# Router logits taken ahead of the norm, stage tiles laid out as views of one room, and three expert panels loaded to other places

## The chip, the cores and the metric

One Trainium2 chip, one of its cores. The metric is the device time of one execution in microseconds (us). TensorE is called PE here, VectorE DVE, ScalarE ACT and SyncE SP; SP issues every DMA of this kernel, all on one queue.

## The reference, cut to what matters

The program is one transformer block with a mixture of experts, followed by two further layers. The change lies in the first block, with 256 tokens of width 1024:

```
x  = x + g1 * (m @ w_out)                  # m: the three branches, gated and merged
h2 = rms_norm(x, norm2_g) * (1 + sc2) + sh2
aff = softmax(h2 @ w_router)               # 256 tokens x 16 experts
top_w, top_i = top_k(aff.T, 32)            # every expert takes 32 tokens
xg = h2[top_i]
y  = (silu(xg @ w_gate) * (xg @ w_up)) @ w_down      # per expert
x  = x + g2 * scatter_add(y * top_w)
```

The two further layers (w_ada, w_ff1, ...) are untouched. All data is float32.

## The kernel before, in words

Everything is kept transposed: `xT` holds 8 tiles of 128 features by 256 tokens. Each engine has its own instruction list, written out in order, and waits on semaphores. A stage ends with a barrier of all engines.

**project_out** (lines 982 to 1145) merges the branches and applies `w_out`. PE makes 4 branch panels (L1071); DVE gates and adds them into `merged` (L1131 to L1137) and counts `bank_free`, which reaches 4 when the last gate is used. Then PE makes 8 chunks of the projection (L1770, 16 matrix instructions each), and DVE adds each into `xT` (L1777, count `x_updated`). PE's chunk q may start when chunk q-2 has been added. Between these additions DVE works on eight **side panels** (L1110 to L1117) of 1 MB each, which belong to the modulation of the next layer: the panel of number 4+q stands in DVE's list behind the addition of chunk q. SP loads them into three buffers (L1020), so panel 6 is issued when panel 3 is used up. After the last chunk come the norm's sum (L1651, L1653), the root on ACT (L1625), the reciprocal and scaling on DVE (L1668, L1674), the shift on ACT (L1659) and the router's logits on PE (L1086).

**moe** (line 1173 on) has 16 experts of 12 panels, each panel 2 MB of weights, 192 in all: 8 up panels (L1282) and 4 down panels (L1307) each. The first two panels lie in lead slots (`x_sel`'s room and `second_panel`), and 8 ring slots take the others in turn, so 10 panels fit before one has been used. `second_panel` is loaded once more. After that the panel of number r can be loaded when panel r-8 has been used. The opening is a chain: PE turns h (L1339), DVE and ACT make the softmax, DVE finds each expert's tokens (L1498 to L1512), PE gathers the tokens of four experts (L1355), and then the first up panel may start. The other experts' tokens are gathered between the up panels of the first expert (L1368); between its down panels PE makes 8 turns of the combine weights (L1332), each copied out by DVE (L1530) before the next.

## Time and profile before

| | |
|---|---|
| device time, median of 3 runs | 2592.0 us (2591.82 to 2593.31) |
| device time of the profiled execution | 2592.07 us |
| its span, first to last instruction | 2590.3 us |
| mean granted PE clock | 0.933 of 2.4 GHz |
| busy: PE, DVE, ACT | 2199.1, 1045.4, 470.3 us |
| DMA | 721.52 MB, mean 279 GB/s |
| issue of the router's load, SP L1024 | 256.51 us |
| span of the output projection's 8 chunks | from 281.94 us to 315.33 us |

Busy times of different engines overlap and say nothing of the end by themselves; which wait ends last in a stage is read from the timeline and the waits.

### The profile page before, as it was taken

The numbers are of one execution on the slowest core, as the hardware profiler recorded it, in microseconds if no ns is written. First come the engines' busy times: TensorE is split into PE (matmuls) and PEld (weight loads), VectorE is DVE, ScalarE is ACT, GpSimd is POOL, SyncE is SP. The second block draws the span as 40 slices with busy tenths as digits, with TensorE's granted clock in tenths as the row PEclk, the third lists the DMA queues.
The fourth block names the chain that finished last, engine by engine and source line by source line (L and its number), as shares of the span: only waits on it lengthen the run. The fifth ranks groups of instructions, "written<-read, shape, count | busy, mean of one in ns | idle before, by whom it ended". The sixth has DMA issues, their size and how long they took to land. (4 is left out here: it accounts for less than half of the span.)

```text
span 2590.3 us, 29682 instructions
## 1 busy us (share of the span) xinstructions
PE 2199.1 (85%) x11896; PEld 1519.2 (59%) x11896; DVE 1045.4 (40%) x1840; ACT 470.3 (18%) x1049; POOL 6.1 (0%) x11
## 2 busy tenths in 40 slices
PE   8999887566655565665899999999999999999998
PEld 5786742111111111111588886888888888778887
DVE  5753631000000100000587457576338754756531
ACT  3204110000000000000222045322112203442220
POOL 0000000000000000000000000000000000000000
PEclk9999988878888888778899999999999999999999
DMA  9653789999999999999977531076447663106430
GB/s 391 232 215 134 303 351 418 428 427 428 429 427 427 429 428 427 428 428 427 420 282 314 223 117 71 2 320 266 178 163 302 277 261 125 69 22 244 163 130 17
DMA packets 75202, 721.52 MB, mean 279 GB/s; under 512 B 8657, under 2 KB 11729, under 8 KB 13521
## 3 DMA queue, kind: packets, MB, share of 16 engines
q1 hardware_dynamic: 75088, 719.95, 67.8%
q8 instruction: 78, 1.28, 0.2%
q14 instruction: 36, 0.29, 0.0%
HBM read 718.87 MB, written 1.05 MB: 278 GB/s over the span
## 5 line engine op out<-in xcount | busy, mean ns | idle before, releaser
L1282 PE MATMUL bank<-pool,moe_x_cur 128*32 128x512 f32 x1776 | 266.3, 737 | 146.8 <-DMA pool<-in_w_expert 146.8
L1770 PE MATMUL bank<-trunk_proj,pool 128*128 128x256 f32 x1408 | 309.1, 379 | 0.0
L1770 PEld LDWEIGHTS bank<-trunk_proj,pool 128*128 128x128 f32 x1408 | 265.5, 190 | 37.5 <-issue 2.5
L1282 PEld LDWEIGHTS bank<-pool,moe_x_cur 128*32 128x32 f32 x1776 | 54.4, 122 | 344.6 <-DMA pool<-in_w_expert 238.8
L1307 PE MATMUL bank<-pool,moe_hidT 128*32 128x512 f32 x864 | 143.8, 802 | 72.7 <-DMA pool<-in_w_expert 65.2
L1468 DVE TENSOR_TENSOR moe_hid<-bank,moe_silu 128x512 f32<-128x512 f32 x16 | 11.1, 691 | 449.9 <-ACT moe_silu L1424 449.9
L1848 PE MATMUL bank<-pool 128*128 128x256 f32 x640 | 152.1, 381 | 0.0
L1848 PE MATMUL bank<-spare,trunk_mix 128*128 128x256 f32 x640 | 146.7, 382 | 3.6 <-ACT first_layer_sq L1907 3.6
L2156 PE MATMUL bank<-pool 128*128 128x256 f32 x672 | 148.3, 380 | 0.0
L1848 PE MATMUL bank<-pool,trunk_mix 128*128 128x256 f32 x640 | 145.7, 381 | 0.0
L2156 PEld LDWEIGHTS bank<-pool 128*128 128x128 f32 x672 | 127.2, 190 | 21.2 <-issue 4.2
L1848 PEld LDWEIGHTS bank<-spare,trunk_mix 128*128 128x128 f32 x640 | 122.6, 192 | 20.9 <-issue 4.0
L1848 PEld LDWEIGHTS bank<-pool,trunk_mix 128*128 128x128 f32 x640 | 122.5, 191 | 17.0
L1307 PEld LDWEIGHTS bank<-pool,moe_hidT 128*32 128x32 f32 x864 | 28.0, 131 | 172.8 <-DMA pool<-in_w_expert 105.6
L787 PE MATMUL bank<-pool 128*128 128x256 f32 x576 | 126.8, 379 | 1.0 <-PEq L2926 1.0
L1848 PEld LDWEIGHTS bank<-pool 128*128 128x128 f32 x640 | 117.6, 190 | 17.2 <-issue 3.3
L787 PEld LDWEIGHTS bank<-pool 128*128 128x128 f32 x576 | 109.2, 190 | 19.1 <-issue 4.7
L1472 DVE COPY moe_y<-bank 128x512 f32<-128x512 f32 x16 | 11.1, 691 | 264.4 <-PE bank L1307 247.8
L1424 ACT ACTIVATE moe_silu<-bank 128x512 f32<-128x512 f32 x16 | 9.6, 597 | 567.3 <-PE bank L1282 567.3
L1321 PE MATMUL bank<-moe_place,moe_y 128*128 (+1 forms) x256 | 70.1, 422 | 43.7 <-DVE xT L1481 26.3
L1777 DVE SCALAR_TENSOR_TENSOR xT<-bank,gain,xT 128x256 f32<-128x256 f32 x32 | 15.5, 484 | 214.8 <-PE bank L1770 214.8
L1321 PEld LDWEIGHTS bank<-moe_place,moe_y 128*128 128x128 f32 x256 | 50.4, 207 | 76.4 <-DVE xT L1481 33.2
(647 smaller groups left out, 2876.2 us busy)
## 6 DMA issues: line engine op xcount, KB each, us to landing
pool<-in_w_expert SPq DMA_DIRECT2D x165, 2048.0 KB, 35.7
pool<-in_w_ff SPq DMA_DIRECT2D x132, 1024.0 KB, 6.9
pool<-in_w_ada SPq DMA_DIRECT2D x66, 1024.0 KB, 8.9
moe_more<-in_w_expert SPq DMA_DIRECT2D x23, 2048.0 KB, 37.0
pool<-in_w_in SPq DMA_DIRECT2D x40, 1024.0 KB, 5.1
pool<-in_w_mod SPq DMA_DIRECT2D x24, 1024.0 KB, 7.8
pool<-in_w_out SPq DMA_DIRECT2D x10, 1024.0 KB, 10.4
pool<-in_small SPq DMA_DIRECT2D x2, 2560.0 KB, 9.4
```

The source lines that it names most:

```text
L787: mm = pe.matmul(ps[p % 3][:, j * T:(j + 1) * T], w[:, j * KD + k], h[:, k], start=k == 0, stop=k == KD - 1)
L1282: mm = pe.matmul(ps[b][quarter[g], :], x_cur[:, u], w[:, b, g], start=u == 0, stop=u == up_panels - 1)
L1307: mm = pe.matmul(ps[2 + b][quarter[g], :], hidT[:, s, g], w[:, g, b], start=s == 0, stop=s == down_panels - 1)
L1321: mm = pe.matmul(ps[at][:, (j % 2) * T:(j % 2 + 1) * T], y[:, k * P:(k + 1) * P], place_of[:, e], start=True, stop=True)
L1424: sc.activation(silu, ps[0], ACT.Silu).then_inc(silu_done, 1)
L1468: ve.tensor_tensor(hid, ps[1], silu, MUL).then_inc(hid_done, 1)
L1472: ve.tensor_copy(y[:, 512:D], ps[3]).then_inc(y_high, 1)
L1770: mm = pe.matmul(self.ps[3 + q % 2][:, 0:T], w, x[:, k], start=k == 0, stop=k == nk - 1)
L1777: ve.scalar_tensor_tensor(self.xT[:, q], self.ps[3 + q % 2][:, 0:T], gain[:, q:q + 1], self.xT[:, q], MUL, ADD).then_inc(self.x_updated, 1)
L1848: mm = pe.matmul(bank, left[:, k], right[:, k], start=start and k == 0, stop=k == 3, skip_group_check=True)
L2156: mm = pe.matmul(ps[n % 3][:, j * T:(j + 1) * T], slot[:, j * KD + k], hT[:, k], start=k == 0, stop=k == KD - 1)
```

## The change

1. **project_out.** The router works on `x * gain`, which DVE writes as each chunk is added (`dve_lead`); the logits of features 0 to 3 stand in PE's list behind chunk 4, the others behind chunk 7. The token's 1/rms and the shift's part of the logits are applied later, to 16 numbers a token. The sum of squares goes to a column per token (8 small matrix instructions of one column). The router's load is issued first. ACT takes one square root early, and loads the table for Exp at the end.
2. **Room.** The tiles of front, project_in, project_out and moe are views of one tile, `room`. This frees the places of `x_sel` and `more` when the gates are merged, and two panels (0 and 9) are loaded there inside project_out, at `bank_free` 4, ahead of side panels 6 and 7 in SP's list.
3. **moe.** An eleventh panel (number 10) goes into h's buffer when h has been turned. The reload of `second_panel` becomes number 11. The tokens and h are scaled and shifted where they are copied out. The combine weights are no longer spread fourfold by ACT: PE's turns of them become 16 matrix products with 32-column weights, in place of 4 transposes. Two copies of the affinities are left out (DVE reads PSUM).

```diff
@@ project_out, SP
+                sp.dma_start(router, I["small1"][:, SM1["router"][0]:SM1["router"][1]]).then_inc(router_here, 16)
                 for n in range(len(side)):
                     side_panel(n)
-                sp.dma_start(router, I["small1"][:, SM1["router"][0]:SM1["router"][1]]).then_inc(router_here, 16)
...
                     if u == 3:
+                        sp.wait_ge(d.bank_free, panels)
+                        for slot, n, here in early_panels:
+                            sp.dma_start(slot, I["w_expert"][0, n]).then_inc(here, 16)
                         for n in range(len(side) + panels - 1, 8):
                             side_panel(n)
@@ project_out, PE
+                def logits(k):
+                    pe.wait_ge(d.led, k + 1)
+                    for t in range(NT):
+                        pe.matmul(ps[t][:, 0:E], h[:, k, t * P:(t + 1) * P], router[:, k * E:(k + 1) * E],
+                                  start=k == 0, stop=k == KD - 1)
...
+                    if q == 4:
+                        for k in range(4):
+                            logits(k)
+                for k in range(4, KD - 1):
+                    logits(k)
+
+                pe.wait_ge(d.folded, 6)
+                pe.wait_ge(d.squared, KD)
+                for t in range(NT):
+                    col = slice(t * P, (t + 1) * P)
+                    pe.matmul(ps[6][:, t:t + 1], d.rstd[:, col], c["ones"][:, 0:1], start=True, stop=False)
+                    mm = pe.matmul(ps[6][:, t:t + 1], d.sq[:, 3, col], c["ones"][:, 0:1], start=False, stop=True)
+                mm.then_inc(d.summed, 1)
+                logits(KD - 1)
@@ project_out, ACT and DVE
-                d.act_norm(sc, 0, mod[:, 24:32, 0], 1)
+                sc.wait_ge(d.summed, 1)
+                sc.activation(root, ps[6][:, 0:NT], ACT.Sqrt, bias=c["eps"][:, 0:1], scale=1.0 / D).then_inc(d.rooted, 1)
+                sc.activation(folded_shift[:, 0:NT], c["eps"][:, 0:NT], ACT.Exp)
-                    d.dve_add(ve, q, 0, mod[:, 16:24, 0], d, 0)
+                    d.dve_add(ve, q, 0, mod[:, 16:24, 0], d, 0, gain[:, 2])
-                d.dve_norm(ve, 0, gain[:, 2])
@@ moe
-                sp.dma_start(lead_slots[0], src[0, 0]).then_inc(lead_here[0], 16)
-                for u in range(6, slots):
-                    sp.dma_start(slot[u], src[0, u + leads]).then_inc(slot_loaded[u], 16)
+                sp.dma_start(slot[6], src[0, 6 + leads]).then_inc(slot_loaded[6], 16)
+                sp.wait_ge(h_turned, 4)
+                sp.dma_start(h_room, src[0, in_h]).then_inc(h_room_here, 16)
                 sp.wait_ge(panel_done, 2)
                 sp.dma_start(second_panel, src[0, again]).then_inc(second_here, 16)
                 for r in range(again + 1, 2 * n):
-                    sp.wait_ge(panel_done, r - slots if r <= again + slots else r - slots + 1)
+                    sp.wait_ge(panel_done, r - slots - 1 if r <= again + slots else r - slots + 1)
...
-                        mm = pe.transpose(ps[7][:, j * P:(j + 1) * P],
-                                          w_tok[:, j % 2, 2 * g + j // 2].rearrange("p a b -> p (a b)"), c["ident"])
+                        for rows in quarter:
+                            mm = pe.matmul(ps[7][rows, j * P:(j + 1) * P], w_tok[:, j % 2, 2 * g + j // 2], c["ident"],
+                                           start=True, stop=True)
...
-                ve.tensor_copy(affT, ps[1][0:E, 0:T])
-                link(ve.tensor_copy(left, ps[1][0:E, 0:T]))
```

The helper that `gain[:, 2]` switches on, unchanged in the file:

```
    def dve_add(self, ve, q, n, gain, norm, m, lead_gain=None):
        if q >= 2 and lead_gain is not None:
            norm.dve_fold(ve, m, q - 1)
        self.dve_update(ve, q, n, gain)
        if lead_gain is not None:
            ve.wait_ge(self.x_updated, n + q + 1)
            norm.dve_lead(ve, q, lead_gain)
```

On SP, in project_out from the first expert panel to the end of the stage, before and after (`room` is where the side panels' tiles, and now two expert panels, lie; `in_w_ada` is the side panels' source, `in_w_expert` the experts'):

```order
L1039 DMA pool<-in_w_expert 128x4096
L1020 DMA mixer_proj<-in_w_ada 128x2048
L1020 DMA mixer_spec<-in_w_ada 128x2048
L1020 DMA pool<-in_w_ada 128x8x256
L1039 DMA pool<-in_w_expert 128x4096 x2
L1020 DMA mixer_proj<-in_w_ada 128x2048
L1020 DMA mixer_spec<-in_w_ada 128x2048
L1039 DMA pool<-in_w_expert 128x4096 x3
```

```order
L1046 DMA pool<-in_w_expert 128x4096
L1024 DMA first_room<-in_w_ada 128x2048 x2
L1024 DMA pool<-in_w_ada 128x8x256
L1046 DMA pool<-in_w_expert 128x4096 x2
L1040 DMA first_room<-in_w_expert 128x4096 x2
L1024 DMA first_room<-in_w_ada 128x2048 x2
L1046 DMA pool<-in_w_expert 128x4096 x3
```

Two loads of 2 MB (L1040) now stand between the panels issued at 282.30 us and side panels 6 and 7.

On PE, from the projection's chunk 3 to the end of the stage before, and to the sum of squares now (L1770 and L1811 are the same chunks, 8 products each; L1086 and L1072 the logits; L1651, L1653 and L1107, L1108 the sum of squares; L1096 the shift's part of the logits):

```order
L1770 MATMUL bank<-pool 128x256 x32
L1049 MATMUL bank<-mixer_kv,ones 32x256 x4
L1770 MATMUL bank<-pool 128x256 x8
L1651 MATMUL bank<-pool,ones 128x256
L1653 MATMUL bank<-pool,ones 128x256
L1059 MATMUL bank<-ident,project_out_rows 128x128 x2
L1086 MATMUL bank<-first_router,pool 128x16 x16
```

```order
L1811 MATMUL bank<-pool 128x256 x8
L1096 MATMUL bank<-pool,ones 128x16
L1811 MATMUL bank<-pool 128x256 x8
L1072 MATMUL bank<-first_router,pool 128x16 x8
L1811 MATMUL bank<-pool 128x256 x16
L1056 MATMUL bank<-first_room,ones 32x256 x4
L1811 MATMUL bank<-pool 128x256 x8
L1066 MATMUL bank<-ident,project_out_rows 128x128 x2
L1072 MATMUL bank<-first_router,pool 128x16 x6
L1107 MATMUL bank<-ones,pool 128x1
L1108 MATMUL bank<-ones,pool 128x1
```

Half of the 16 products of the logits moved between chunk 4 and chunk 5. Six stand behind chunk 7; then the pair L1107, L1108 comes for each of two tiles of tokens, and the last two products follow.

On PE, in the first expert's down panels, before and now (L1307 and L1346 are the panels, L1332 and L1372 the turns of the combine weights, two turns each row):

```order
L1307 MATMUL bank<-pool,moe_hidT 32x512 x8
L1332 MATMUL bank<-ident,pool 128x128 x8
L1307 MATMUL bank<-moe_more,moe_hidT 32x512 x8
L1332 MATMUL bank<-ident,pool 128x128 x8
L1307 MATMUL bank<-spare,moe_hidT 32x512 x8
```

```order
L1346 MATMUL bank<-pool,first_room 32x512 x8
L1372 MATMUL bank<-ident,first_room 32x128 x32
L1346 MATMUL bank<-first_room 32x512 x8
L1372 MATMUL bank<-ident,first_room 32x128 x32
L1346 MATMUL bank<-pool,first_room 32x512 x8
```

Each pair of turns went from 8 instructions to 32; the third panel is now the one in h's buffer.

## Rows read from the trace of the kernel before

**Rows 1.** The page, GB/s of DMA in 40 equal slices of the span
```profile
GB/s 391 232 215 134 303 351 418 428 427 428 429 427 427 429 428 427 428 428 427 420 282 314 223 117 71 2 320 266 178 163 302 277 261 125 69 22 244 163 130 17
```

**Rows 2.** Windows: stretch, its us, busy us by engine, PEclk, DMA share, GB/s
```profile
400.00:405.00 5.00, 5.00 (x49) 1.59 (x52) 1.66 (x4) 0.00 (x0) 0.00 (x0) 1.00 0.83 288
405.00:1245.00 840.00, 514.05 (x3099) 139.53 (x3092) 66.56 (x142) 32.01 (x60) 0.00 (x0) 0.82 1.01 428
345.00:350.00 5.00, 4.63 (x36) 1.90 (x38) 1.66 (x3) 3.02 (x3) 0.00 (x0) 1.00 0.02 7
```

**Rows 3.** Longest of PE's waits inside the expert stage, 405 to 1245 us
```profile
PE bank L1282 <- DMA pool<-in_w_expert: 146.8, 67, 3.0
```

**Rows 4.** Timeline of SP's issues around the output projection
```profile
282.30 1.13 SPq L1039 DMA_DIRECT2D pool<-in_w_expert  x2
288.60 0.33 SPq L1020 DMA_DIRECT2D mixer_proj<-in_w_ada  x1
...
298.62 17.55 SPq L1039 DMA_DIRECT2D pool<-in_w_expert  x3
```

**Rows 5.** DMA issues of 288.4 to 291.2 us: KB each, us to landing
```profile
mixer_proj<-in_w_ada SPq DMA_DIRECT2D x1, 1024.0 KB, 12.3
```

**Rows 6.** DMA issue of 283.0 us alone, then that of 298.6 us
```profile
pool<-in_w_expert SPq DMA_DIRECT2D x1, 2048.0 KB, 15.4
...
pool<-in_w_expert SPq DMA_DIRECT2D x1, 2048.0 KB, 9.6
```

**Rows 7.** Timeline of DVE, 300 to 304 us
```profile
300.89 1.28 DVE L1114 SCALAR_TENSOR_TENSOR mixer_kv<-mixer_proj,cond,mixer_kv 128x1024 f32<-128x1024 f32 x1 [5.11 <-DMA mixer_proj<-in_w_ada]
...
303.41 0.48 DVE L1777 SCALAR_TENSOR_TENSOR xT<-bank,first_mod,xT 128x256 f32<-128x256 f32 x1
```

**Rows 8.** Timeline of PE from chunk 0 of the projection to the expert stage
```profile
286.12 4.58 PE L1770 MATMUL bank<-pool 128*128 128x256 f32 x20 [1.42 <-DVE pool L1137]
...
303.94 7.17 PE L1770 MATMUL bank<-pool 128*128 128x256 f32 x32 [1.89 <-DVE xT L1777]
...
311.61 3.72 PE L1770 MATMUL bank<-pool 128*128 128x256 f32 x16
...
321.09 6.98 PE L1086 MATMUL bank<-first_router,pool 128*128 128x16 f32 x32 [3.49 <-ACT pool L1659]
328.36 3.29 PE L1339 MATMUL bank<-ident,pool 128*128 128x128 f32 x16 [0.30 <-PEq L1007]
```

**Rows 9.** Timeline of ACT, 328 us
```profile
328.32 1.28 ACT L1437 ACT_TABLE_LOAD   x1 [4.40 <-PEq L1007]
```

**Rows 10.** Windows of PE's lower clock, columns as in Rows 2
```profile
320.90:331.20 10.30, 9.81 (x46) 9.77 (x47) 3.40 (x13) 5.89 (x17) 0.00 (x0) 0.50 0.76 285
...
339.40:344.80 5.40, 5.35 (x25) 5.38 (x26) 2.04 (x4) 0.28 (x1) 0.00 (x0) 0.50 0.98 422
```

**Rows 11.** Timeline of DVE in the routing
```profile
330.54 0.37 DVE L1495 TENSOR_SCALAR moe_aff<-moe_e,moe_tot 128x16 f32<-128x16 f32 x2
331.91 0.41 DVE L1498 COPY moe_y<-bank 16x256 f32<-16x256 f32 x1 [1.00 <-PE bank L1344]
...
332.69 0.42 DVE L1501 MAX8 moe_best<-moe_y 16x8 f32<-16x256 f32 x1
...
338.81 1.43 DVE L1512 TENSOR_TENSOR moe_place<-moe_placeT,moe_numbers 128x128 f32<-128x128 f32 x4
```

**Rows 12.** Timeline of PE, first panel of the first expert
```profile
346.18 1.92 PE L1282 MATMUL bank<-moe_x_sel,moe_x_cur 128*32 128x512 f32 x16 [0.37 <-ACT moe_x_cur L1445]
```

**Rows 13.** DMA issue of 315.7 us: KB, us to landing
```profile
pool<-in_w_expert SPq DMA_DIRECT2D x1, 2048.0 KB, 13.5
```

**Rows 14.** Timeline of PE in the first expert's down panels
```profile
380.57 0.66 PE L1332 MATMUL bank<-ident,pool 128*128 128x128 f32 x4 [0.78 <-DVE moe_place L1530]
```

**Rows 15.** PE and its weight loads with 32-column weights
```profile
290.63 0.64 PE L1049 MATMUL bank<-mixer_proj,ones 128*32 128x256 f32 x8
...
346.18 0.16 PEld L1282 LDWEIGHTS bank<-moe_x_sel,moe_x_cur 128*32 128x32 f32 x8 [0.56 <-ACT moe_x_cur L1445]
```

More of the change, by code:

```diff
@@ L992, in project_out @@
         merging, router_here, gain_squared = st.sem("merging"), st.sem("router_here"), st.sem("gain_squared")
+        shift_rows, shift_sum, shift_made = st.sem("shift_rows"), st.sem("shift_sum"), st.sem("shift_made")
+        d.lead, d.led_before = h, {0: 0}
+        by_shift = d.silu[:, 0, 0:KD * E].rearrange("p (k e) -> p k e", k=KD)
+        folded_shift, root = d.silu[:, 1, 0:E], d.root[:, 0:NT]
         panels, x_gain = 4, t["x_gain"]
@@ L1147, in _ @@
                         tile_add(0)
-                d.dve_norm(ve, 0, gain[:, 2])
                 tile_add(1)
+                ve.wait_ge(d.rooted, 1)
+                ve.reciprocal(route["rstd"], root)
 def head_rows_of(extra):
@@ L1173, in moe @@
 def moe(nc, c, ps, cst, hT, place_of, x_sel, slot, slot_loaded, src, xT, gate, pool, w_ff, ff_here, x_gain, second_panel,
-        second_here, ff_mod, ff_gain, final_g):
+        second_here, ff_mod, ff_gain, final_g, route, shift, lead_sem, take):
     up_panels, down_panels = KD, 4
@@ L1187, in moe @@
         e1 = st.sb("e1", [P, NT, E])
+        logits = st.sb("logits", [P, NT, E])
         top = st.sb("top", [P, NT])
@@ L1271, in panel @@
                         return second_panel
-                    if opening and r < again:
+                    if opening and r == in_h:
+                        pe.wait_ge(h_room_here, 16)
+                        return h_room
+                    if opening and r < in_h:
                         pe.wait_ge(slot_loaded[r - leads], 16)
                         return slot[r - leads]
-                    pe.wait_ge(slot_loaded[slot_of(r)], i * (32 * n // slots) + ((r - leads - 1) // slots + 1) * 16)
+                    pe.wait_ge(slot_loaded[slot_of(r)], i * (32 * n // slots) + ((r - leads - 2) // slots + 1) * 16)
                     return slot[slot_of(r)]
@@ L1420, in tokens, with middle @@
                     sc.activation(x_cur, xs[:, :, e], ACT.Copy).then_inc(x_ready, 1)
-                def middle(e, more):
+                def middle(e, more, opening=False):
                     sc.wait_ge(panel_done, e * n + up_panels)
@@ L1432, in middle @@
                     sc.wait_ge(panel_done, e * n + n)
+                    if opening:
+                        sc.wait_ge(w_turned, E // 2)
                     sc.activation(y[:, 0:512], ps[2], ACT.Copy).then_inc(y_low, 1)
                 for t in range(NT):
-                    sc.wait_ge(highest, NT)
-                    sc.activation(e1[:, t], ps[t][:, 0:E], ACT.Exp, bias=top[:, t:t + 1],
+                    sc.wait_ge(highest, 1)
+                    sc.activation(e1[:, t], logits[:, t], ACT.Exp, bias=top[:, t:t + 1],
                                   accum_out=tot[:, t:t + 1]).then_inc(exped, 1)
@@ L1489, in _ @@
                 for t in range(NT):
-                    ve.tensor_reduce(top[:, t:t + 1], ps[t][:, 0:E], AX.X, MAX, negate=True).then_inc(highest, 1)
+                    m = ve.scalar_tensor_tensor(logits[:, t], ps[t][:, 0:E], route["rstd"][:, t:t + 1], route["shift"], MUL, ADD)
+                link(m)
+                ve.tensor_reduce(top, logits, AX.X, MAX, negate=True).then_inc(highest, 1)
                 link(ve.memset(zero, 0.0))
@@ L2790, with __init__ @@
 class Spectrum:
-    def __init__(self, st, c, ps, cst, src, vec, spec):
+    def __init__(self, st, c, ps, cst, src, vec, spec, take):
         self.c, self.ps, self.cst, self.src, self.vec, self.spec = c, ps, cst, src, vec, spec
-        self.small = st.sb("small", [P, SM1["router"][0]])
-        self.feats = st.sb("feats", [P, T])
-        self.window = st.sb("window", [P, NT, T])
-        self.dft = st.sb("dft", [P, 4, 640])
-        self.masked = st.sb("masked", [P, P])
-        self.h1 = st.sb("h1", [HEAD, T])
-        self.ang = st.sb("ang", [HEAD, T])
-        self.tmp = st.sb("tmp", [HEAD, T])
-        self.filt = st.sb("filt", [P, NT, 2, 512])
-        self.size = st.sb("size", [P, NT, 2, 512])
-        self.norm = st.sb("norm", [P, 512])
+        self.small = take(SM1["router"][0])
+        self.feats = take(T)
+        self.window = take(NT, T)
+        self.dft = take(4, 640)
+        self.masked = take(P)
+        self.h1 = take(T, rows=HEAD)
+        self.ang = take(T, rows=HEAD)
+        self.tmp = take(T, rows=HEAD)
+        self.filt = take(NT, 2, 512)
+        self.size = take(NT, 2, 512)
+        self.norm = take(512)
         self.first_here, self.later_here, self.layer, self.angled, self.sined = (
@@ L2896, in dve_divide, with front @@
             ve.tensor_tensor(self.spec[:, f], self.ps[1 + f], self.norm, MUL)
-def front(nc, c, ps, ring, extra, I, cst, vec, cond, xT, ctxT, hT, mod, gain, spec, slots, loaded, consts, consts_here):
+def front(nc, c, ps, ring, extra, I, cst, vec, cond, xT, ctxT, hT, mod, gain, spec, slots, loaded, consts, consts_here, take):
     v = lambda k: vec[:, V1[k][0]:V1[k][1]]
```

117 lines of the change are left out of this document (64 added, 53 removed).

## The prediction

> **What bounds the kernel now.** I read the page first: from slice 7 to slice 20, near half the span, DMA moves 418 to 429 GB/s [rows 1]. So I cut the expert stage into windows: from 405 to 1245 us the DMA share is 1.01 at 428 GB/s, while PE is busy for 514 of 840 us [rows 2], and the longest of PE's waits there is for expert panels, 146.8 us in 67 waits [rows 3]. A panel of 2,097,152 bytes costs 2.097 / 0.428 = 4.9 us of that stream. The 192 panels pass through a fixed number of places, so time is lost or won only where the stream pauses or starts. It starts in the stage's opening, when 10 panels are loaded and the first has not been used: between 345 and 350 us it moves 7 GB/s [rows 2]. There is a second weak spot, 400 to 405 us with 288 GB/s. The load of panel 20 may be issued only when panel 12 has been used, the first of the second expert, and so behind the whole first expert on PE. Every microsecond by which PE comes later to panel 12 moves the rest of the stream, and the end, by one microsecond. I therefore followed PE and what it waits for from the output projection to there.
>
> **The two early panels.** SP issued two expert panels at 282.30 and 283.0 us, side panel 6 at 288.60 [rows 4]. The second of the two landed 15.4 us after its issue, at 298.4 [rows 6], side panel 6 12.3 us after its own, at 300.9 [rows 5], the panel issued at 298.62 9.6 us later, at 308.2 [rows 6]. All land in the order of issue, and back to back. DVE stood 5.11 us for side panel 6 and began with it at 300.89 [rows 7]. Behind it in DVE's list is the addition of chunk 3, which ended at 303.89, and PE's chunk 5 waits for that: it began at 303.94 [rows 8]. Now two panels of 4.9 us are issued at `bank_free` 4, just ahead of 286.12, where PE's wait on DVE's last gate ends [rows 8]; side panel 6 still waits for panel 3's use, to 288.6. So it stands behind 9.8 us more of DMA and lands at 310.7.
> From there: side panel 6 on DVE 2.6 us (300.89 to the addition's 303.41 is 2.52) to 313.3; `dve_add` now folds a square first and writes `dve_lead` afterwards. The trace ahead of the change has no lead here; I price fold and lead as the addition beside them, 0.48 each at most [rows 7], pipelined to some 0.4. The addition ends at 314.2, lead 3 at 314.6. Logits 0 to 2 fit into PE's wait; those of feature 3 do not, 4 instructions of 6.98 / 32 = 0.22 us [rows 8], 0.9 us. Chunk 5 begins at about 315.5, **11.5 us later**. In that gap PE would have little to do. After its thin stretch ahead of 320.9 the granted clock was 0.50 (1.2 GHz), for 10.3 us; in the gather it came back 5.4 us after 339.4 [rows 10]. I take 5.4 us at half speed, which costs 2.7 us (bounds: 0 without a fall, 5.2 with 10.3 us of it). Chunks 5 to 7 took from 303.94 to 315.33 [rows 8]; so chunk 7 ends at 315.5 + 11.4 + 2.7 = 329.5, 14.2 later.
>
> **The norm's tail.** From 315.33 to the first instruction of moe at 328.36 were 13.0 us: sum, root, reciprocal, scaling, shift, 32 instructions of logits [rows 8]. What remains: one turn of 0.35, 12 instructions of logits, 8 of the column sums, a root of 128x2, then on ACT the table load of 1.28, which stood in moe at 328.32 [rows 9], and an Exp of 0.3. The 0.22 us of a product with 128-column weights was at clock 0.50 [rows 8, 10]; behind three busy chunks I take 0.11. So 0.35 + 12 x 0.11 + 8 x 0.11 + 0.2 + 0.3 + 1.28 + 0.3, and 0.2 for the barrier, is 4.8 us (at the lower clock 7.0). The saving is 8.2 us. moe starts at 334.3, **6.0 later**.
>
> **The opening of moe.** The affinities were ready at 330.91 and PE's 16 transposes of h, 3.29 us at the lower clock, held them up until 331.6; then two copies ran from 331.91 to the first MAX8 at 332.69 [rows 8, 11]. The copies go: 0.8 us. The table load is gone ahead of the Exp; with the transposes at full clock (1.8 us) the affinities go through 1.0 us sooner, at the lower clock not at all. I take 1.8 together. Against it: `numbers` was used at 338.81 [rows 11], and its load now queues behind the panels issued at chunk 7's end. The second of that pair landed 13.5 us after its issue [rows 13]: 329.8 + 13.5 = 343.3, where DVE wants it at 334.3 + 10.5 - 1.8 = 343.0. I take 0.5 us (bounds 0 and 1.5). The first up panel, 346.18 before [rows 12], comes 6.0 - 1.8 + 0.5 = **4.7 later**, at 350.9. Additions and scalings that replace copies (`x_cur`, `x_sel`, h's copy) have the shapes of the copies; I give them nothing, for DVE is busy there for 1.66 of 5 us [rows 2], and ACT's four copies of h end long before the gather. ACT's spread lay beside PE's up panels; its absence brings nothing.
>
> **The turns of the combine weights.** A turn of 4 transposes took 0.66 us, and the next waits 0.78 for DVE's copy [rows 14]; all 8 stand in PE's chain to panel 12. Now 32 instructions with 32-column weights. The nearest rows: 16 such instructions of 512 columns take 1.92 us [rows 12], 8 of 256 columns 0.64 [rows 15]. Four run together, so these are 4 rounds and 2 rounds; a line through both gives 0.21 us plus 0.83 ns a column, so 8 rounds of 128 columns take 1.07. That is 0.41 more each, **3.3 us** for eight. The bounds: nothing (as now) and 32 x 0.08 = 2.6 us each, if an instruction costs what it does in the 256-column row whatever its length, 15 us more in all.
> A rule speaks for something like the upper bound. The Trainium skill (TensorE: Matmul & The Clock Gate, Part 3: Packing small matmuls) says that weight loads overlap running matmuls only when the row group differs; these quarters differ in columns only. By it 32 loads of 0.106 us would stand in line and a turn would be an estimated 3.4 us. The trace does not agree: 8 loads of this kind lie within 0.16 us [rows 15].
>
> **The eleventh panel.** It would take 4.9 us off the stream if the stream ran on. But panels 11 to 19 now fill the 9 places that come free early, and panel 20 still waits for panel 12. From panel 2's use to the end of 19 are 9 panels instead of 10, so the pause ahead of 20 grows by the 4.9 us that were won. I count nothing. The later issue of the feed-forward panels at the stage's end (the turn of the slots shifts by one) I count at nothing too: they queue behind the last expert panels, which PE itself still waits for.
>
> **The sum.** 11.5 + 2.7 - 8.2 - 1.8 + 0.5 + 3.3 = 8.0 us later at panel 12, and so at the end. The profiled execution took 2592.07 around a span of 2590.3; the median is 2592.0. Forecast: **2600 us**.
>
> **Rivals.**
> (a) The side panels are not held up. If the DMA engines let the 1 MB loads past, chunk 5 starts at about 305.0 (fold, lead, logits of feature 3), chunk 7 ends at 316.4, moe starts at 321.2, the first up panel at 337.8, 8.4 earlier, and with 3.3 for the turns the end is 5.1 earlier: 2587. For it speaks only that 16 engines each work on their own share, of which these landings show the last alone; against it, that each load of these 25 us landed in the order of issue [rows 4 to 6]. It decides from this point: if side panel 6 comes less than about 5 us later, the change does not lose. By the Trainium skill (DMA: Bandwidth & Descriptors, Queues, rings and completion order) an engine takes up descriptors in ring order; by that rule, the trace agrees. Chance 0.07.
> (b) The stream and not PE decides at panel 20. Then the eleventh panel counts: 4.7 - 4.9, no change, 2592. Against it: panel 2 is used some 5 us after 350.9, panel 19 lands 9 x 4.9 us and a start of 2 or 3 later, at some 403 us; the load of 20 was issued in the weak spot from 400 to 405 us [rows 2], and PE now gets there 8 us later. Chance 0.08.
> (c) PE's clock stays up through the wait, or comes back before the gather: the 2.7 falls away, and the gather of 6.4 us at the lower clock halves. 2594 to 2597. Chance 0.18.
> (d) A turn costs an instruction's 0.08 or the rule's load 32 times: 2600 + 12 to + 19, 2612 to 2619. Chance 0.06.
> The forecast's own course has 0.61.
>
> **Range.** The forecast's own bounds: clock -2.7 and +2.5, tail +2.2, numbers -0.5 and +1.0, not all at once: 2595 to 2606. With (c), and the lower side for (b), 2592 to 2606 holds 8 in 10. A measurement of this kernel tells about 0.2%, 5.2 us. Faster by that needs (a) at its full size: 0.06. Within it lie (b), most of (c) and the low edge of the forecast: 0.24. Slower: 0.70.
>
> **What would show it.** Of the kernel after: DVE waits some 15 us for side panel 6 and starts it near 310.7; PE's chunk 5 begins near 315, at clock 0.50; from chunk 7's end to moe 5 us; the first up panel near 351; a turn of 32 instructions near 1.1 us; DMA nearly still for 6 to 7 us ahead of panel 20, and 428 GB/s from there. Wrong would be: side panel 6 at its old time, a DMA without that pause, or turns of over 1.5 us.

## The result, and the profile after

| | before | after |
|---|---|---|
| median of 16 runs each | 2592.53 us (2587.83 to 2594.64) | 2598.29 us (2597.17 to 2601.74) |
| span of the profiled execution | 2590.3 us | 2596.5 us |

The ratio is 1.0027, with a 95% interval from 1.002 to 1.0033: the change makes the kernel slower by 5.8 us. Measured again (e11 below), the same two kernels gave 1.003 (1.0018 to 1.0042). The forecast was 2600.0 us.

The page of the kernel after, GB/s of DMA in 40 slices. The plateau of 427 to 428 stands where it stood, with the same height; the slices ahead of it changed (351 and 418 were slices 6 and 7 in [rows 1], now 341 and 369), and so did those behind its end:

```profile
GB/s 391 232 213 136 320 341 369 427 427 428 428 428 428 428 428 428 428 428 427 420 302 291 250 114 73 2 307 266 190 162 292 278 262 130 65 26 243 163 130 17
```

SP's issues, timeline (start, length, queue, line). The pair of L1040 stands ahead of the two side panels of L1024, which are issued at the time of [rows 4]:

```profile
282.42 1.13 SPq L1046 DMA_DIRECT2D pool<-in_w_expert  x2
286.21 0.81 SPq L1040 DMA_DIRECT2D first_room<-in_w_expert  x2
288.73 3.10 SPq L1024 DMA_DIRECT2D first_room<-in_w_ada  x2
298.75 31.84 SPq L1046 DMA_DIRECT2D pool<-in_w_expert  x3
```

DMA issues of 288.5 to 289 us: KB each, us to landing. It was 12.3 in [rows 5]:

```profile
first_room<-in_w_ada SPq DMA_DIRECT2D x1, 1024.0 KB, 22.3
```

DVE's timeline. The number in brackets is the wait ahead of the instruction; it was 5.11 in [rows 7]. Behind the side panel come the addition of chunk 3 (L1818) and the scaled copy for the router (L1727):

```profile
311.10 1.28 DVE L1143 SCALAR_TENSOR_TENSOR first_room<-first_room,cond 128x1024 f32<-128x1024 f32 x1 [15.15 <-DMA first_room<-in_w_ada]
...
313.96 0.48 DVE L1818 SCALAR_TENSOR_TENSOR xT<-bank,first_mod,xT 128x256 f32<-128x256 f32 x1
314.48 0.35 DVE L1727 TENSOR_SCALAR pool<-xT,first_gain 128x256 f32<-128x256 f32 x1
```

PE's timeline over the same stretch, to the first up panel:

```profile
302.23 1.41 PE L1072 MATMUL bank<-first_router,pool 128*128 128x16 f32 x12
314.88 1.04 PE L1072 MATMUL bank<-first_router,pool 128*128 128x16 f32 x4 [11.24 <-DVE pool L1727]
315.76 9.78 PE L1811 MATMUL bank<-pool 128*128 128x256 f32 x32
...
326.03 3.72 PE L1811 MATMUL bank<-pool 128*128 128x256 f32 x16
...
329.81 1.41 PE L1072 MATMUL bank<-first_router,pool 128*128 128x16 f32 x12
...
334.21 3.17 PE L1379 MATMUL bank<-ident,pool 128*128 128x128 f32 x16 [1.65 <-PEq L1011]
...
344.61 5.61 PE L1395 MATMUL bank<-first_room 128*128 128x128 f32 x32 [0.91 <-DVE first_room L1548]
350.60 1.92 PE L1321 MATMUL bank<-first_room,moe_x_cur 128*32 128x512 f32 x16 [0.38 <-DVE moe_x_cur L1558]
```

PE stands 11.24 us for the copy, starts chunk 5 at 315.76 (before: 303.94), and chunks 5 and 6 take 9.78 us where they took 7.17 [rows 8]. Chunk 7 ends at 329.75, moe starts 4.46 us later. The first window below shows why the two chunks are slow (columns: us; busy us of PE, PEld, DVE, ACT, POOL; granted clock; DMA share; GB/s): the clock is at its lower level, 0.50 or 1.2 GHz, for 13.7 us, from 3.8 us into PE's wait on. The second window shows the pause ahead of panel 20, the third the stream behind it:

```profile
307.40:321.10 13.70, 6.22 (x17) 5.14 (x18) 7.71 (x12) 2.49 (x5) 0.00 (x0) 0.50 0.65 272
...
404.00:410.00 6.00, 4.86 (x36) 2.37 (x40) 2.74 (x7) 0.00 (x0) 0.00 (x0) 1.00 0.00 0
409.00:1250.00 841.00, 522.23 (x3116) 140.35 (x3108) 66.61 (x142) 32.02 (x60) 0.00 (x0) 0.81 1.01 427
```

ACT's timeline at the end of the output projection: root, table load and Exp end at 333.9, and the barrier lets moe start at 334.21. DVE's timeline in moe follows, where `numbers` is first used at L1548, with no wait ahead of it:

```profile
332.14 0.26 ACT L1129 ACTIVATE pool<-bank,eps 128x2 f32<-128x2 f32 x1 [1.41 <-PE bank L1108]
332.42 1.28 ACT L1130 ACT_TABLE_LOAD   x1
333.71 0.20 ACT L1130 ACTIVATE pool<-eps 128x2 f32<-128x2 f32 x1
```

```profile
337.84 0.42 DVE L1537 MAX8 moe_best<-bank 16x8 f32<-16x256 f32 x1 [1.63 <-PE bank L1384]
...
343.96 1.43 DVE L1548 TENSOR_TENSOR first_room<-moe_placeT,moe_numbers 128x128 f32<-128x128 f32 x4
```

PE's timeline in the first expert's down panels (L1346) with the turns (L1372), and the first half of the tokens' return (L1360):

```profile
383.73 1.08 PE L1372 MATMUL bank<-ident,first_room 128*32 128x128 f32 x32 [0.81 <-DVE first_room L1571]
384.63 1.90 PE L1346 MATMUL bank<-first_room 128*32 128x512 f32 x16
386.35 1.06 PE L1372 MATMUL bank<-ident,first_room 128*32 128x128 f32 x32
...
389.12 1.90 PE L1346 MATMUL bank<-pool,first_room 128*32 128x512 f32 x16
...
399.88 3.51 PE L1360 MATMUL bank<-first_room 128*128 128x256 f32 x8 [1.61 <-DVE first_room L1506]
```

The same stretch in the kernel before (L1307 are the down panels, L1321 the tokens' return):

```profile
375.68 3.52 PE L1307 MATMUL bank<-pool,moe_hidT 128*32 128x512 f32 x16 [0.69 <-ACT moe_hidT L1431]
...
381.16 1.92 PE L1307 MATMUL bank<-moe_more,moe_hidT 128*32 128x512 f32 x16
...
385.04 1.92 PE L1307 MATMUL bank<-spare,moe_hidT 128*32 128x512 f32 x16
...
394.45 1.97 PE L1321 MATMUL bank<-moe_place,moe_y 128*128 128x256 f32 x8 [1.58 <-DVE moe_y L1472]
```

A turn takes 1.08 us (0.66 in [rows 14]), but two panels follow each other 4.49 us apart instead of 3.88, so a turn costs the chain 0.3 us. Panel 20 was issued at 409.05 and landed 8.9 us later, at 417.9; before it was issued at 402.07 and landed at 410.0. Panel 19 had landed at 404.0, and at 404.4 before: the stream hardly paused before (5.5 us between the two landings, 4.9 is back to back) and clearly does now (13.9 us).

Two executions of one kernel do not agree in every stage. A second profile of the kernel after (e11 below) begins with the same instructions at the same times, but its clock is at the lower level from 36.6 to 43.4 us, and from 40 us on it runs 3.0 to 3.2 us later:

```profile
36.60:43.40 6.80, 6.10 (x23) 2.70 (x24) 3.28 (x12) 2.67 (x7) 0.00 (x0) 0.50 1.01 416
```

The first profile has 1.00 there. Of the 13 profiles, those of e4, e8 and e11 have this stretch (6.8 us) and those of e1 and e7 half of it (3.4 us, 1.3 us later from there on). It lies in the first stage, far ahead of project_out and moe. Where experiments are compared, times are therefore also given from **the gate**, the start of PE's row behind its wait for DVE's last gate (286.12 in [rows 8], at the end of chunk 0; 286.24 in the kernel after, 289.40 in e11).

### The profile page after: what moved, and what is told of

It reads as the page before. It is cut to its first block and busy times, and to the rows that moved or that the text cites. A ratio compares the mean times of both kernels' runs of the same rounds, so it can differ in the third digit from the quotient of the medians.

```text
span 2596.5 us, 30125 instructions
## 1 busy us (share of the span) xinstructions
PE 2204.2 (85%) x12126; PEld 1521.0 (59%) x12126; DVE 1045.7 (40%) x1843; ACT 464.6 (18%) x1039; POOL 6.1 (0%) x11
## 5 line engine op out<-in xcount | busy, mean ns | idle before, releaser
L1321 PE MATMUL bank<-pool,moe_x_cur 128*32 128x512 f32 x1776 | 265.7, 735 | 138.7 <-DMA pool<-in_w_expert 138.7
L1811 PE MATMUL bank<-trunk_proj,pool 128*128 128x256 f32 x1408 | 309.1, 379 | 0.0
L1811 PEld LDWEIGHTS bank<-trunk_proj,pool 128*128 128x128 f32 x1408 | 265.5, 190 | 37.5 <-issue 2.5
L1321 PEld LDWEIGHTS bank<-pool,moe_x_cur 128*32 128x32 f32 x1776 | 54.2, 122 | 333.8 <-DMA pool<-in_w_expert 227.8
L1346 PE MATMUL bank<-pool,first_room 128*32 128x512 f32 x864 | 146.2, 815 | 71.5 <-DMA pool<-in_w_expert 63.4
L1502 DVE TENSOR_TENSOR first_room<-bank,first_room 128x512 f32<-128x512 f32 x16 | 11.1, 691 | 448.0 <-ACT first_room L1464 448.0
L2197 PEld LDWEIGHTS bank<-pool 128*128 128x128 f32 x672 | 127.2, 190 | 21.2 <-issue 4.2
L1346 PEld LDWEIGHTS bank<-pool,first_room 128*32 128x32 f32 x864 | 28.1, 132 | 173.1 <-DMA pool<-in_w_expert 108.2
L1506 DVE COPY first_room<-bank 128x512 f32<-128x512 f32 x16 | 11.1, 691 | 266.1 <-PE bank L1346 249.5
L1464 ACT ACTIVATE first_room<-bank 128x512 f32<-128x512 f32 x16 | 9.6, 597 | 565.1 <-PE bank L1321 565.1
L1360 PE MATMUL bank<-first_room 128*128 (+1 forms) x256 | 71.8, 430 | 43.7 <-DVE xT L1515 26.3
L1818 DVE SCALAR_TENSOR_TENSOR xT<-bank,gain,xT 128x256 f32<-128x256 f32 x32 | 15.5, 484 | 214.7 <-PE bank L1811 214.7
L1360 PEld LDWEIGHTS bank<-first_room 128*128 128x128 f32 x256 | 51.5, 211 | 77.8 <-DVE xT L1515 33.4
```

What stands on the lines that cost most here:

```text
L1321: mm = pe.matmul(ps[b][quarter[g], :], x_cur[:, u], w[:, b, g], start=u == 0, stop=u == up_panels - 1)
L1346: mm = pe.matmul(ps[2 + b][quarter[g], :], hidT[:, s, g], w[:, g, b], start=s == 0, stop=s == down_panels - 1)
L1360: mm = pe.matmul(ps[at][:, (j % 2) * T:(j % 2 + 1) * T], y[:, k * P:(k + 1) * P], place_of[:, e], start=True, stop=True)
L1464: sc.activation(silu, ps[0], ACT.Silu).then_inc(silu_done, 1)
L1502: ve.tensor_tensor(hid, ps[1], silu, MUL).then_inc(hid_done, 1)
L1506: ve.tensor_copy(y[:, 512:D], ps[3]).then_inc(y_high, 1)
```

## The experiments

Eleven kernels ran, the last of them the kernel after again. The median of the kernel before beside them was 2590.9 us for the first eight and 2592.0 us for the last three. Read from one profile each, in us from the gate:

| | first up panel | issue of panel 20 | landing of panel 22 | last instruction |
|---|---|---|---|---|
| before | 60.1 | 116.0 | 133.6 | 2304.2 |
| after | 64.4 | 122.8 | 141.5 | 2310.3 |
| e11, after again | 63.8 | 120.7 | 139.4 | 2310.2 |
| e1 | 54.0 | 112.6 | 131.2 | 2302.0 |
| e2 | 59.2 | 117.5 | 136.0 | 2304.8 |
| e3 | 64.2 | 122.8 | 141.3 | 2312.1 |
| e4 | 63.8 | 118.1 | 136.7 | 2306.5 |
| e5 | 54.7 | 95.2 | 122.8 | 2294.4 |
| e6 | 64.4 | 104.8 | 132.5 | 2304.1 |
| e7 | 54.1 | 100.8 | 127.2 | 2298.4 |
| e8 | 53.1 | 93.6 | 124.6 | 2296.2 |
| e9 | 67.2 | 125.7 | 144.4 | 2314.9 |
| e10 | 52.7 | 94.8 | 120.9 | 2292.9 |

**The place of the early panels.** In e1_behind both stand behind side panels 6 and 7, in e2_half one ahead and one behind. The edit of e1:

```diff
                     if u == 3:
-                        sp.wait_ge(d.bank_free, panels)
-                        for slot, n, here in early_panels:
-                            sp.dma_start(slot, I["w_expert"][0, n]).then_inc(here, 16)
                         for n in range(len(side) + panels - 1, 8):
                             side_panel(n)
+                        sp.wait_ge(d.bank_free, panels)
+                        for slot, n, here in early_panels:
+                            sp.dma_start(slot, I["w_expert"][0, n]).then_inc(here, 16)
```

> The changed kernel with one edit: SP issues the two early expert panels behind side panels 6 and 7 instead of ahead of them. Theory A (the early panels hold up side panel 6, and PE's arrival at panel 12 sets the end): DVE starts side panel 6 near 301 us instead of 311, the projection's chunk 5 starts near 305, the first up panel near 338, the load of panel 20 is issued near 396 us instead of 409, and the time falls by about 13 us, to 2585 to 2587, 5 to 7 us below the kernel before. Theory B (the expert stream itself decides, and the early panels' place matters little): within 2 us of the changed kernel's 2598.

> The changed kernel with one of the two early panels ahead of side panels 6 and 7 and the other behind them: half the dose. Theory A: side panel 6 lands 4.9 us earlier than in the changed kernel, near 306 us, chunk 5 starts near 310.5, and the time is about 5 us less plus what the clock gives back (0 to 3 us): 2590.5 to 2593.5. Theory B: 2597 to 2599. If the loss were a matter of the two panels' contention and not of their place in line, the time would stay near 2598 too.

Measured: e1 2588.44 us (2585.37 to 2591.36), ratio 0.999 (0.9981 to 0.9999); e2 2595.09 us (2592.08 to 2595.47), ratio 1.0014 (1.0005 to 1.0023). DVE's wait in e1, then PE's first work of chunk 5 and the gather:

```profile
302.48 1.28 DVE L1143 SCALAR_TENSOR_TENSOR first_room<-first_room,cond 128x1024 f32<-128x1024 f32 x1 [5.22 <-DMA first_room<-in_w_ada]
```

```profile
306.98 8.57 PE L1811 MATMUL bank<-pool 128*128 128x256 f32 x32
...
334.49 6.71 PE L1395 MATMUL bank<-first_room 128*128 128x128 f32 x32 [0.90 <-DVE first_room L1548]
341.58 1.92 PE L1321 MATMUL bank<-first_room,moe_x_cur 128*32 128x512 f32 x16 [0.38 <-DVE moe_x_cur L1558]
```

The same wait in e2:

```profile
306.19 1.28 DVE L1144 SCALAR_TENSOR_TENSOR first_room<-first_room,cond 128x1024 f32<-128x1024 f32 x1 [10.19 <-DMA first_room<-in_w_ada]
```

DVE waits 5.22, 10.19 and 15.15 us with no, one and two panels ahead: 5.0 us each, the time of 2 MB. From the gate the issue of panel 20 comes after 112.6, 117.5 and 122.8 us, 4.9 and 5.3 apart. So the order in SP's list is the cause of the loss: with it put right, the rest of the change is worth some 2.5 us by both medians and ratio, with an interval from 0.3 to 4.9. e1 gave back 10 us where 13 were expected, and missed its range of 2585 to 2587 by 1.4 us. Most of the rest is the clock: chunks 5 and 6 of e1 still took 8.57 us, 1.4 more than before, and its gather 6.71, 1.1 more than the 5.61 of the kernel after. e2 missed its range by 1.6 us: by the ratios it is 3.4 us below the kernel after and not 5, though its profile shows the 5 us at panel 20.

**The eleventh panel and the turns.** e3_no_eleventh reloads `second_panel` for panel 10, as before. e4_no_eleventh_old_turns also has the 4 transposes a turn and ACT's spread.

```diff
@@ e3
-        in_h = leads + slots
-        again = in_h + 1
+        again = leads + slots
...
-                sp.wait_ge(h_turned, 4)
-                sp.dma_start(h_room, src[0, in_h]).then_inc(h_room_here, 16)
...
@@ e4, further
...
-                        for rows in quarter:
-                            mm = pe.matmul(ps[7][rows, j * P:(j + 1) * P], w_tok[:, j % 2, 2 * g + j // 2], c["ident"],
-                                           start=True, stop=True)
+                        mm = pe.transpose(ps[7][:, j * P:(j + 1) * P],
+                                          w_tok[:, j % 2, 2 * g + j // 2].rearrange("p a b -> p (a b)"), c["ident"])
...
```

> The changed kernel without the eleventh panel: nothing is loaded into h's buffer, panel 10 goes to second_panel again as in the kernel before, the rest of the change stays. Theory A (the load of panel 20 waits for PE at panel 12, so an eleventh place only lengthens the pause ahead of 20): no change, 2597 to 2599.5, with the stream's pause ahead of panel 20 shorter by about 4.9 us. Theory B (each place ahead takes a panel of 4.9 us off the stream): 2603.

> As e3_no_eleventh, and the combine weights are spread fourfold by ACT and turned by 4 transposes as in the kernel before. Theory A with the turns' price of 0.42 us each: PE is 3.4 us sooner at panel 12; panel 19 lands near 409 us, so the stream allows 3 to 4 us: 2594 to 2595.5, 3 to 4 us below e3_no_eleventh. If the turns are hidden (the rival): equal to e3_no_eleventh within 1 us.

Measured: e3 2600.18 us (2599.53 to 2601.6), ratio 1.0037 (1.0023 to 1.0051); e4 2596.7 us (2592.85 to 2598.29), ratio 1.0019 (1.001 to 1.0028). The window of e3 ahead of panel 20, columns as above, against 0 GB/s in the kernel after:

```profile
404.00:410.00 6.00, 4.89 (x36) 2.37 (x40) 2.71 (x7) 0.00 (x0) 0.00 (x0) 1.00 0.49 202
```

In e3 panel 19 lands at 409.1 instead of 404.0, but panel 20 is issued at 409.0 and lands at 417.7 instead of 417.9: the eleventh place only lengthens the pause. The median of e3 lies 0.7 us above its range of 2597 to 2599.5 and 2 us above the kernel after; the landings do not show this, and the intervals of the two ratios overlap. In e4 a turn's row is 0.66 us again, and the four down panels with their turns take 15.6 us (382.48 to 398.07) instead of the 18.1 of the kernel after (380.12 to 398.27). The new turns cost 2.5 us in all. The medians of e3 and e4 are 3.5 us apart, and panel 20's issue 4.6 us from the gate, but the clock has a part in this: the first down panel of e3 took 3.51 us at the lower clock, that of e4 1.92.

```profile
389.65 0.66 PE L1366 MATMUL bank<-ident,pool 128*128 128x128 f32 x4 [0.79 <-DVE first_room L1570]
390.24 1.92 PE L1341 MATMUL bank<-spare,first_room 128*32 128x512 f32 x16
```

**Reusing the places.** If the pause ahead of panel 20 is where the extra places go lost, their reload should bring them back. In e5_behind_reuse (with e1's order) h's buffer takes panel 20 when panel 10 has been used, `second_panel` takes 21 when 11 has been used, and the ring goes on with 22. e6_reuse is this edit without e1's order.

```diff
...
+                sp.wait_ge(panel_done, in_h + 1)
+                sp.dma_start(h_room, src[ring // n, ring % n]).then_inc(h_room_here, 16)
+                sp.wait_ge(panel_done, again + 1)
+                sp.dma_start(second_panel, src[(ring + 1) // n, (ring + 1) % n]).then_inc(second_here, 16)
+                for r in range(ring + 2, 2 * n):
+                    sp.wait_ge(panel_done, r - slots - 1)
...
```

> e1_behind with one edit more: panels 20 and 21 go once more into h's buffer and second_panel (free when panels 10 and 11 are used), so the load of 20 no longer waits for PE at panel 12; the ring slots go on from panel 22. Theory A (in e1_behind the stream stands idle ahead of panel 20 because the place comes free only with panel 12): panel 21 lands near 405 us and 22 near 410, instead of 418.8 for panel 22 in e1_behind, the pause is gone, and the time falls by 8 to 9 us, to 2579 to 2581. Rival (the pause is harmless, or PE is the bound in the second expert): within 2 us of e1_behind's 2588.4.

> The changed kernel with that edit alone; the early panels stay ahead of the side panels. Theory A: panel 22 lands near 418.5 us instead of 427.7, and the time is 9 us below the changed kernel's, 2589 to 2590, no slower than the kernel before although PE is as late as ever. Rival: 2597 to 2599.

Measured: e5 2582.89 us (2580.12 to 2585.8), ratio 0.997 (0.9958 to 0.9982), the lowest time so far; e6 2592.08 us (2590.1 to 2595.81), ratio 1.0004 (0.9995 to 1.0013). Windows of e5: the stream runs through where e1 and the kernel after stood still.

```profile
390.00:396.00 6.00, 4.00 (x10) 2.75 (x11) 1.66 (x4) 0.00 (x0) 0.00 (x0) 0.72 1.02 434
396.00:402.00 6.00, 6.00 (x52) 2.55 (x54) 1.66 (x4) 0.00 (x0) 0.00 (x0) 1.00 1.04 429
```

In e1, whose gate lies 1.3 us later, 6 us out of the same stretch:

```profile
394.00:400.00 6.00, 4.25 (x31) 2.16 (x33) 3.32 (x8) 0.00 (x0) 0.00 (x0) 1.00 0.01 3
```

From the gate, panel 22 landed after 122.8 us in e5 and 131.2 in e1, after 132.5 in e6 and 141.5 in the kernel after: 8.4 and 8.9 us sooner, about as theory A had it. The end came 7.6 and 6.2 us sooner in the profiles, and in time the reload is worth 5 us from e1 to e5 and 6 us from the kernel after to e6, each by the ratios times 2592. That is less than the 8 to 9 us expected, and both runs lie some 2 us above their ranges. What was given back between panel 22 and the end was not traced. Without the reload the eleventh place showed nothing (e3).

**What each place is then worth.** e7_behind_reuse_no_eleventh is e5 without the eleventh panel. e8_no_early_reuse is e5 with the two early panels loaded when moe starts.

```diff
@@ e7, on e5: h's buffer takes no panel
-                sp.wait_ge(h_turned, 4)
-                sp.dma_start(h_room, src[0, in_h]).then_inc(h_room_here, 16)
...
@@ e8, on e5
...
-                        for slot, n, here in early_panels:
-                            sp.dma_start(slot, I["w_expert"][0, n]).then_inc(here, 16)
...
+                sp.dma_start(lead_slots[0], src[0, 0]).then_inc(lead_here[0], 16)
+                for u in range(6, slots):
+                    sp.dma_start(slot[u], src[0, u + leads]).then_inc(slot_loaded[u], 16)
```

> e5_behind_reuse without the eleventh panel: panel 10 goes to second_panel, which is loaded a third time with panel 19; nothing lies in h's buffer. Theory A: the stream has no pause in either, so here, unlike in e3_no_eleventh, the eleventh place counts as one panel of the stream: 4.9 us above e5_behind_reuse, 2584 to 2586. Rival (the eleventh place is worth nothing at all): equal to e5_behind_reuse within 1 us.

> As e5_behind_reuse, but panels 0 and 9 are not loaded early: they go to the same places at the start of the expert stage, as in the kernel before. Theory A: the stream still carries them between 327 and 352 us, where it otherwise stands nearly still, panel 11 lands near 357 us instead of 354.6, and the time is 2 to 3 us above e5_behind_reuse: the two early panels are worth far less than their 9.8 us. Rival: 9 to 10 us above e5_behind_reuse.

Measured: e7 2586.0 us (2580.7 to 2588.03), ratio 0.9974 (0.9965 to 0.9984); e8 2585.68 us (2582.33 to 2587.05), ratio 0.9978 (0.9969 to 0.9987). From the gate, panel 22 lands after 122.8 us in e5, 127.2 in e7 and 124.6 in e8. The eleventh panel is worth 4.4 us of landing and 4.0 us at the end of the profile, the early loads 1.7 and 1.8 us. In time they are 3.1 and 2.8 us by medians, 1.0 and 2.1 us by the ratios; the intervals of e5, e7 and e8 overlap, so the times do not show the size of either, and it rests on one profile of each.

**The clock and the wait.** e9_busy_wait puts 40 products on PE into its wait for side panel 6; e10_busy_opening puts 5 and 18 on e5's PE, in the barrier's wait and in the routing's. e11_after_again is the kernel after, unedited.

```diff
@@ e9
                     if q == 4:
-                        for k in range(4):
+                        for k in range(3):
                             logits(k)
+                        for _ in range(40):
+                            pe.matmul(ps[6][:, 0:T], c["ident"], merged[:, 0], start=True, stop=True)
+                        logits(3)
@@ e10, on e5, behind the last logits and behind the transposes of the affinities
+                for _ in range(5):
+                    pe.matmul(ps[5][:, 0:T], c["ident"], xT[:, 0], start=True, stop=True)
...
+                for _ in range(18):
+                    pe.matmul(ps[7][:, 0:T], c["ident"], xT[:, 0], start=True, stop=True)
```

> The changed kernel, with 40 extra products (128 rows by 256 columns, result not used) on PE inside its 11.2 us wait, ahead of the logits of feature 3. Theory (the thin stretch of PE sets the granted clock back, and the lower clock costs time in chunks 5 and 6 and later in the routing): the products run 302.9 to some 312, chunks 5 and 6 take 7.2 us instead of 9.8, the lower clock at 307.4 is gone, moe and the first up panel come 2.6 us earlier (348.0), the end some 2.6 us earlier: about 2595.5 where the changed kernel gives 2598. Rival (the granted clock falls by its own course, whatever PE does): chunks 5 and 6 still 9.8, time as before. Side panel 6 lands at 311.1 in both.

> The kernel with the early panels behind side panels 6 and 7 and the two reloads (2582.9), with extra products on PE whose result is not used: 5 behind the last logits of the output projection (in the barrier's wait) and 18 in PE's 5.5 us wait of the routing. Theory (the granted clock follows how busy PE is): the transposes of h take 1.8 instead of 2.8 us, the gather some 3 instead of 6.0, the first up panel comes 3 to 4 us earlier, at 337.5, and the end at about 2579.5. Rival (PE has to be busy for longer than these 6 us before the clock rises, or the extra products themselves run at the lower clock and then reach into the chain): 18 products at half speed take 8.3 us instead of the wait's 5.5, so the gather starts up to 2.8 us later: 2583 to 2586.

> The changed kernel itself, unedited, beside the other two on one chip: 2597 to 2599 by all theories; it is the base for the difference of the run with the busy wait.

Measured: e9 2603.02 us (2601.12 to 2604.03), ratio 1.0043 (1.0029 to 1.0057); e10 2582.34 us (2580.93 to 2583.98), ratio 0.9966 (0.9954 to 0.9978); e11 2599.6 us (2598.0 to 2601.42), ratio 1.003 (1.0018 to 1.0042). PE in e9:

```profile
303.57 17.51 PE L1101 MATMUL bank<-pool,ident 128*128 128x256 f32 x80
320.93 0.52 PE L1072 MATMUL bank<-first_router,pool 128*128 128x16 f32 x4
321.29 7.15 PE L1814 MATMUL bank<-pool 128*128 128x256 f32 x32
...
337.12 2.39 PE L1382 MATMUL bank<-ident,pool 128*128 128x128 f32 x16 [1.65 <-PEq L1011]
```

Here I sized the edit wrong. A product in float32 is two rows of the trace (x80 for 40), 0.44 us, so the products ran 17.5 us and not 9, and chunk 5 began 5.5 us later than in the kernel after. The run is useful all the same: chunks 5 and 6 take 7.15 us instead of 9.78, the lower clock of 307.4 us is gone, and all five profiles with PE's wait of 11 us and nothing in it (the kernel after, e3, e4, e6 and e11) have these chunks slow, 8.55 to 9.95 us. That speaks for the wait as what brings the lower clock; it is one profile of e9, and e10 below shows that the clock is not settled by PE's work alone. The sum 5.5 - 2.6 = 2.9 us is met: moe starts at 337.12 instead of 334.21 (from the gate 3.3 us later than in e11), and the median is 3.4 above e11. So a delay of PE ahead of the first expert shows at the end at about its size.

PE in e10, where the same error made the 18 products reach past DVE's result:

```profile
325.66 7.93 PE L1408 MATMUL bank<-xT,ident 128*128 128x256 f32 x36
333.52 0.29 PE L1411 MATMUL bank<-ident,first_room 16*128 16x16 f32 x2
334.72 3.81 PE L1418 MATMUL bank<-first_room 128*128 128x128 f32 x32 [0.90 <-DVE first_room L1571]
```

From moe's start the turn of the places came 1.4 us later than in e5 (10.1 us instead of 8.7), the gather took 3.81 instead of 5.97 us, and the first up panel came 0.8 us sooner. Against it, the 5 products in the barrier's wait took 3.58 us, most of it at the lower clock, and moe began 2.1 us later behind the last logits than in e5. In time the whole is nothing that the runs tell from e5, and neither the 2579.5 of the theory nor the rival's 2583 to 2586 was met. Whether fewer products would bring more was not tried.

The same two profiles show something else. Ahead of the 5 products at 319.5 us PE's instructions are the same in e5 and e10, and so is PE's wait of 1.3 us ahead of the logits of feature 3. Chunks 5 and 6 took 10.15 us in e5 and 7.15 in e10:

```profile
305.77 10.15 PE L1830 MATMUL bank<-pool 128*128 128x256 f32 x32
```

```profile
305.47 7.15 PE L1834 MATMUL bank<-pool 128*128 128x256 f32 x32
```

In e1, e7 and e8, with the same wait, they took 8.57, 8.65 and 8.84 us. So the same work on PE met either level of the clock, and up to 3 us of a difference between two profiles can be this.

## Why the prediction was right

The change loses 5.8 us where 8.0 were forecast, and on the path that was forecast: the early panels hold up side panel 6, PE comes later to panel 12, and the stream restarts later. The terms one by one:

**Where the time goes.** That the stream restarts behind PE at panel 20 was right: 0 GB/s for 6 us ahead of it, 427 GB/s after it, and PE still waits for these panels there. Two of PE's longest waits from 409 to 1250 us (us in total, times, longest), the first to be read beside [rows 3]:

```profile
PE bank L1321 <- DMA pool<-in_w_expert: 138.7, 67, 3.0
...
PE bank L1321 <- DMA first_room<-in_w_expert: 33.0, 14, 3.0
```

Panel 20 landed 8.0 us later than before, the stage's last panels 7.0, the span ended 6.2 later, the median 5.8. That the landing meets the forecast's 8.0 to the tenth is luck: the issue was 7.0 us late, and 1.0 came from the restart, which took 8.9 us from issue to landing instead of 7.9 and is not in the sum. What was given back after panel 20 was not traced to a row. Two profiles of this kernel differ by 2.1 us at panel 20's issue from the gate (122.8, and 120.7 in e11), and both end 6.0 to 6.1 us later than before, counted from there.

**The two early panels.** Side panel 6 landed at 311.08 (310.7 predicted), the addition ended at 314.44 (314.2), chunk 5 began at 315.76 (315.5), chunk 7 ended at 329.75 (329.5). The clock's term was 2.7 and measured 2.6 (2.15 in e11); the lower clock lasted 13.7 us, but PE stood still in the first 7.5 of them. Rival (a) fell: all loads of this stretch landed in the order of issue. The Trainium skill (DMA: Bandwidth & Descriptors, Queues, rings and completion order) states that an engine takes up descriptors in ring order, though not that their completions keep it; by that rule the trace agrees, with 5.0 us for each panel ahead in e2 and in the kernel after.

**The norm's tail.** 4.46 us against 4.8: a saving of 8.6 instead of 8.2, so moe started 5.85 later (6.0). It is the largest gain in the change, and the loss by the delayed side panel is larger still.

**The opening.** 1.43 us were saved where 1.8 - 0.5 = 1.3 were counted, but by other parts, so this agreement is luck. The way to the first MAX8 became 0.7 us shorter, not 1.8: PE's transposes stayed at the lower clock (3.17 us) and still held the affinities up. `numbers` was not waited for, so the 0.5 was nil: it landed at 342.45 and was used at 343.96. The gather took 5.61 us instead of the 6.4 before, which was not in the sum. The first up panel came 4.42 later (4.7). Windows of the lower clock in the transposes and around the gather, columns as above:

```profile
334.70:338.10 3.40, 3.10 (x16) 2.53 (x14) 1.17 (x6) 3.10 (x8) 0.00 (x0) 0.51 1.06 453
341.60:348.40 6.80, 4.19 (x20) 4.11 (x21) 4.38 (x12) 0.00 (x0) 0.00 (x0) 0.50 1.02 430
```

**The turns.** The record of a turn is 0.42 us longer, as the line through two rows of [rows 12, 15] had it (0.41). But this is the mis-sized term: I multiplied the record by 8 for 3.3 us, and the chain lost 2.5. By the profile's ends, which are modelled, the first instructions of a turn start while the panel ahead of it still runs (384.63 + 1.90 is 386.53, the turn starts at 386.35; 0.18 us of overlap, 0.07 before), so the spacing of the panels, 0.61 us for two turns, is the cost. Rival (d) fell. The weight loads of a turn lie inside its row of 1.08 us:

```profile
383.73 0.81 PEld L1372 LDWEIGHTS bank<-ident,first_room 128*32 128x32 f32 x32 [1.08 <-DVE first_room L1571]
```

By the rule of the Trainium skill (TensorE: Matmul & The Clock Gate, Part 3: Packing small matmuls), loads overlap running matmuls only when the row group differs, which it does not here; the trace does not agree. The 3.4 us that the prediction made of this rule was also too high an estimate: it took 0.106 us for a load, what one with 128 columns takes in the kernel before (4 in 0.42 us), while 8 loads with 32 columns took 0.16 us [rows 15]. What the rule gives with these loads was not worked out.

**The clock further on.** Not in my sum: before, the first down panel ran at the lower clock (3.52 us instead of 1.92, 375.68 us); after, it did not, but the first return of tokens did (3.51 instead of 1.97), in the first profile and not in e11. So 4.4 + 2.5 - 1.6 + 1.5 = 6.8 of the 7.0 at panel 20's issue, and 3.7 + 2.5 - 1.6 = 4.6 of the 4.8 in e11. At this point the forecast of 8.0 was 1 to 3 us too much, for this and the turns.

**The eleventh panel.** Worth nothing, as counted (e3). Rival (b) fell: what was won ahead of panel 20 went into the pause. With the pause removed it is worth 4.4 us of landing (e5, e7).

**Rival (c).** The clock did fall in the wait. It came back at 321.1 us, fell again for 334.7 to 338.1, and once more at 341.6, 3 us ahead of the gather, to 348.4: so the gather began at the lower clock and ended at the higher, and neither half of the rival came true.

## What to carry to other kernels

In a queue that lands in order, ask of each prefetch not whether its place is free but what small load is issued behind it and who waits for that: 4 MB ahead of a 1 MB panel cost 10 us here, and two exchanged blocks of code got them back. Before reading a difference of 3 us off two profiles, compare the granted clock stretch by stretch, and count from a common instruction behind the last stage that was not changed. A further buffer is worth something only if the load that restarts the stream no longer waits for the same event; find that load, and count from it. Price a burst of small instructions by the distance of the work on both sides of it, not by the length of its row.

## What the runs showed of the hardware

- A turn of 32 rows with 32-column weights took 1.08 us against 0.66 for 4 transposes with 128, and cost 0.3 us between neighbours. Its 32 weight loads took 0.81 us inside this.
- The granted clock of one kernel in two profiles was not the same stretch by stretch: 3.4 us at 0.50 from 399.6 us in the first, none there in the second, which is 1.5 us of PE; none from 36.6 to 43.4 us in the first, 0.50 throughout in the second, which is 3.0 to 3.2 us of the span.
- With the same PE work ahead of them, chunks 5 and 6 took 7.15 us in e10 and 10.15 in e5.
- The stream's restart costs: panel 20 landed 8.9 us after its issue with the DMA idle, while back to back a panel takes 4.9 us.
